# Passing the ends and beginnings of stages one block of 128 tokens at a time, merging by column blocks, and splitting weights in two steps

## The reference, cut to what matters

```python
for l in range(DEPTH):
    mod = silu(c) @ w_mod[l] + b_mod[l]                 # six rows of 1024: shift, scale, gate, twice
    h = rms_norm(x, g_mix_pre[l]) * (1 + sc_mix) + sh_mix
    y = hybrid_mixer(h, ...)                            # below
    x = x + gt_mix * rms_norm(y, g_mix_post[l])
    h = rms_norm(x, g_ffn_pre[l]) * (1 + sc_ffn) + sh_ffn
    y = swiglu(h, ...) if l % 2 == 0 else moe_swiglu(h, ...)   # dense; top 2 of 8 experts
    x = x + gt_ffn * rms_norm(y, g_ffn_post[l])

def hybrid_mixer(h, ...):
    proj = h @ w_in                 # 1024 x 5120: q, k, v of 8 stick-breaking heads, q, k, v of 8
                                    # MoBA heads, two gates of 1024 columns
    o_a = stick_breaking_attention(...) @ w_proj_sb
    o_b = moba_attention(...) @ w_proj_moba
    return (sigmoid(g_a) * o_a + sigmoid(g_b) * o_b) @ w_out
```

## Time and profile before

| | us |
|---|---|
| three runs: lowest, median, highest | 1754.01, 1759.09, 1759.86 |
| the profiled execution, its own time | 1758.54 |
| span in the profile | 1756.8 |
| mean granted share of TensorE's clock | 0.976 |

### The profile page before, as it was taken

The page is one execution under the profiler, slowest core; times in us unless marked ns, Lnnn a source line. Parts: engine busy times, 40 slices in busy tenths (PEclk is TensorE's granted clock), DMA queues, the critical chain, the costliest instruction groups (busy, mean ns, idle before and its releaser), DMA issues.

```text
span 1756.8 us, 23111 instructions
## 1 busy us (share of the span) xinstructions
PE 1667.5 (95%) x8014; PEld 1370.6 (78%) x8014; DVE 1386.9 (79%) x1260; ACT 1108.4 (63%) x965; POOL 62.9 (4%) x194
## 2 busy tenths in 40 slices
PE   6999879999979997799999999999999999999997
PEld 5977668878779776688788788788788788787885
DVE  7867867777685466588888888888888888888888
ACT  4656344334345564477777777777777777778775
POOL 0020010000000101400000000000000000000000
PEclk9999989999989999799999999999999999999998
DMA  9954647776556343189989899899899899899894
GB/s 385 394 203 180 247 165 284 273 266 254 215 210 256 134 149 139 51 309 372 350 342 371 309 358 376 316 365 374 317 373 371 297 373 368 321 375 358 325 370 165
DMA packets 72830, 512.05 MB, mean 291 GB/s; under 512 B 8963, under 2 KB 10188, under 8 KB 10828
## 3 DMA queue, kind: packets, MB, share of 16 engines
q1 hardware_dynamic: 72496, 511.26, 76.6%
q10 hardware_dynamic: 284, 0.13, 0.0%
HBM read 510.30 MB, written 1.06 MB: 291 GB/s over the span
## 4 chain that ended last, share of the span: by engine, by line
PE 85%; DVE 6%; ACT 4%; issue 3%; POOL 1%; DMA 1%; ACTq 0%; DVEq 0%; SPq 0%; POOLq 0%
PE ps L1231 26%; PE ps L1233 25%; PE ps L1232 25%; DVE wlo L291 3%; ACT whi L286 2%; PE ps L1564 2%; PE ps L1453 2%; DMA raw<-in_w_mod_units 1%; PE ps L1320 1%; DVE x L783 1%; ACT L286 1%; PE ps L1588 0%; DVE wide L1031 0%; PE ps L1340 0%; PE ps L1545 0%
## 5 line engine op out<-in xcount | busy, mean ns | idle before, releaser
L291 DVE TENSOR_TENSOR wlo<-raw,whi 128x2048 fp32r<-128x2048 f32 x436 | 993.7, 2290 | 231.2 <-ACT whi L286 229.1
L286 ACT ACTIVATE whi<-raw 128x2048 fp32r<-128x2048 f32 x436 | 833.7, 1916 | 294.0 <-PE ps L1233 293.4
L1231 PE MATMUL ps<-whi,hhi 128*128 128x512 f32 x1376 | 549.3, 399 | 15.3 <-DVE wlo L291 5.3
L1232 PE MATMUL ps<-whi,hlo 128*128 128x512 f32 x1376 | 539.8, 392 | 0.0
L1233 PE MATMUL ps<-wlo,hhi 128*128 128x512 f32 x1376 | 538.6, 391 | 0.0
L1231 PEld LDWEIGHTS ps<-whi,hhi 128*128 128x128 f32 x1376 | 260.5, 189 | 83.7 <-DVE wlo L291 14.2
L1233 PEld LDWEIGHTS ps<-wlo,hhi 128*128 128x128 f32 x1376 | 260.4, 189 | 55.9
L1232 PEld LDWEIGHTS ps<-whi,hlo 128*128 128x128 f32 x1376 | 260.7, 189 | 52.4 <-issue 1.0
L1231 PE MATMUL ps<-whi,ohi 128*128 128x512 f32 x624 | 250.5, 401 | 4.5 <-DVE gate L764 2.0
L1233 PE MATMUL ps<-wlo,ohi 128*128 128x512 f32 x624 | 244.5, 392 | 0.0
L1232 PE MATMUL ps<-whi,olo 128*128 128x512 f32 x624 | 243.8, 391 | 0.0
(11 more groups left out here) (214 smaller groups left out, 1062.4 us busy)
## 6 DMA issues: line engine op xcount, KB each, us to landing
raw<-in_w_moe SPq DMA_DIRECT2D x336, 1024.0 KB, 6.6
raw<-in_w_pre_moe SPq DMA_DIRECT2D x100, 1024.0 KB, 4.9
raw<-in_w_mod_units SPq DMA_DIRECT2D x48, 1024.0 KB, 5.4
x<-in_x SPq DMA_DIRECT2D x1, 1024.0 KB, 5.3
bias<-dist_scratch SPq DMA_DIRECT2D x1, 1024.0 KB, 7.9
out<-x SPq DMA_DIRECT2D x2, 512.0 KB, 2.7
condb<-in_c SPq DMA_DIRECT2D x1, 512.0 KB, 6.7
qk<-in_bucket_onehot ACTq DMA_DIRECT2D x1, 49.4 KB
```

The source lines that it names most:

```text
L286: nc.scalar.activation(whi[:, s % SPLIT, :], raw[:, slot(s), :], ACT.Copy).then_inc(hi_done, 1)
L291: nc.vector.tensor_tensor(wlo[:, s % SPLIT, :], raw[:, slot(s), :], whi[:, s % SPLIT, :].bitcast(F32), ALU.subtract).then_inc(lo_done, 1)
L1231: nc.tensor.matmul(out, a_hi, b_hi, start=first, stop=False, **kw)
L1232: nc.tensor.matmul(out, a_lo, b_hi, start=False, stop=False, **kw)
```

## The change

1. **Splits in two steps.** `split_hi` and `split_lo` do two instructions of 1024 columns instead of one of 2048. `hi_done` and `lo_done` count halves. PE's `use(s)` waits for the first half only, and a new `rest(s)` waits for the second in the middle of the unit's first pass (before the third of four k slices, or the second of two).
2. **Ends of stages by blocks of tokens.** Unit 24 is done for both blocks; then units 25, 26, 27 for block 0, and after that units 25, 26, 27 for block 1. The units of w_out are reordered (k half outside, column half inside). The last down products of the dense FFN are done likewise (`dense_end`), with three units' worth for block 0 and then for block 1; all three slots of whi and wlo are held until block 1 has used them.
3. **Beginnings of stages likewise.** `transposes(n, 0)`, then the first three units of the next stage for block 0, then `transposes(n, 1)`, then the same three units for block 1 (`phase_start`). For this mixer 1 takes its column blocks in the order 2, 6, 0, 1, 3, 4, 5, 7, 8, 9, in pairs of banks. Before the experts only the transposes are apart. ACT, DVE and POOL get one list each for a passage (`transition`), with split halves of the first units of the next stage placed between the pieces of work on each block.
4. **Merge by column blocks.** Units 20 and 21 are the two projections of column half 0, units 22 and 23 those of half 1. Half 0 is transposed after unit 22 and half 1 after unit 24. The four sigmoids are made one after each of the units 19 to 22. Attention steps stand nearer together (`STEP_AT`).
5. **Smaller.** Places of the mod loads in the ring; `gate_take` of the dense FFN at steps 1 and 2 instead of 1 and 3; squares are scaled by 1/32 in the instruction, so that POOL has one multiplication less; the residual add is one instruction of 1024 columns instead of two of 512.

```diff
     for s in range(FIRST, MOE0):
         order.append(("unit", s))
-        if (s < FFN0 and s in (8, 9, 10, 11, 12, 13, 15, 18, 21, 24, 25, 26)
-                or FFN0 <= s < FFN0 + 40 and (s - FFN0) % 2 == 0 or MIX1 < s <= MIX1 + 8):
+        f = s - FFN0
+        if (s in (8, 9, 10, 11, 12, 13, 15, 17, 18, 20, 21, 23)
+                or 0 < f < 38 and (f % 2 == 1 and f > 1 or f in (4, 6)) or MIX1 + 2 < s <= MIX1 + 10):
             order.append(("mod", next(mods)))
     assert next(mods, None) is None
     return order
...
+        def split_hi(act, s, r=0, halves=(0, 1)):
+            if 0 in halves:
+                act.wait_ge(raw_full[slot(s)], dma_value(s, r))
+                wait_at_least(act, unit_used, number(s, r) - SPLIT + 1)
+            for h in halves:
+                part = slice(h * D, (h + 1) * D)
+                nc.scalar.activation(whi[:, s % SPLIT, part], raw[:, slot(s), part], ACT.Copy).then_inc(hi_done, 1)
+
+        def split_lo(dve, s, r=0, halves=(0, 1)):
+            if 0 in halves:
+                wait_at_least(dve, unit_used, number(s, r) - SPLIT + 1)
+            for h in halves:
+                part = slice(h * D, (h + 1) * D)
+                dve.wait_ge(hi_done, number(s, r) * 2 + (h + 1))
+                nc.vector.tensor_tensor(wlo[:, s % SPLIT, part], raw[:, slot(s), part],
+                                        whi[:, s % SPLIT, part].bitcast(F32), ALU.subtract).then_inc(lo_done, 1)
 
...
+        HI = [0, 8, 12]
+        NEXT = [None, FFN0, MIX1, MOE0]
+        T_BANK = [None, (6, 4), (6, 4), (6, 0)]
+        Y_BANK = [(2, 4, 3, 5), (4, 5, 0, 1), (2, 4, 3, 5)]
+        ORDER = [list(range(BLK)), [2, 6, 0, 1, 3, 4, 5, 7, 8, 9]]
+        NEED = [[3, 4, 4, 4, 5, 5, 5, 5], [4, 4, 4, 4, 6, 6, 6, 6]]
+
+
+        STEP_AT = [16, 19, 22, 25, 28, 31, 33, 36, 38, 41]
+
...
+            def transition(q):
+
+                n = q + 1
+                square_y(q, 0)
+                square_y(q, 1)
+                split_hi(act, NEXT[n], halves=(0,))
+                square_x(n, 0)
+                split_hi(act, NEXT[n], halves=(1,))
+                split_hi(act, NEXT[n] + 1, halves=(0,))
+                if q != 1:
+                    square_y(q, 2)
+                hidden_a(n, 0)
+                if n < 3:
+                    hidden_hi(n, 0)
+                if q == 1:
+                    square_y(q, 2)
+                square_y(q, 3)
+                split_hi(act, NEXT[n] + 1, halves=(1,))
+                if n < 3:
+                    split_hi(act, NEXT[n] + 2)
+                square_x(n, 1)
+                hidden_a(n, 1)
+                if n < 3:
+                    hidden_hi(n, 1)
 
...
+            def transition(q):
+
+                n = q + 1
+                coefficients(n)
+                if q == 1:
+                    last_add(0)
+                    last_add(1)
+                gated_y(q, 0)
+                gated_y(q, 1)
+                residual(q, 0)
+                split_lo(dve, NEXT[n], halves=(0,))
+                normed(n, 0)
+                split_lo(dve, NEXT[n], halves=(1,))
+                hidden_b(n, 0)
+                if n < 3:
+                    hidden_lo(n, 0)
+                if q == 1:
+                    last_add(2)
+                    last_add(3)
+                split_lo(dve, NEXT[n] + 1, halves=(0,))
+                gated_y(q, 2)
+                gated_y(q, 3)
+                residual(q, 1)
+                split_lo(dve, NEXT[n] + 1, halves=(1,))
+                if n < 3:
+                    split_lo(dve, NEXT[n] + 2, halves=(0,))
+                normed(n, 1)
+                if n < 3:
+                    split_lo(dve, NEXT[n] + 2, halves=(1,))
+                hidden_b(n, 1)
+                if n < 3:
+                    hidden_lo(n, 1)
...
+                def merge_first(half):
+                    for c in range(C):
+                        dve.wait_ge(sig_done, 4 * l + 2 * half + 1)
+                        dve.wait_ge(unit_used, base + 21 + 2 * half)
+                        nc.vector.tensor_tensor(merged[:, c, half * NB:(half + 1) * NB], bank[4 * half + c][:],
+                                                gates[:, c, half * NB:(half + 1) * NB], ALU.mult).then_inc(mg_evac, 1)
+
+                def merge_second(half):
...
+                for u in range(MIX_UNITS - 2):
+                    if u == 25:
+                        merged_lo(1)
+                    if l and u or u >= FIRST - LEAD:
+                        stream_lo(dve, base + u + LEAD)
                     attention(2 * u)
                     attention(2 * u + 1)
...
+                    if u in (20, 22):
+                        merge_first((u - 20) // 2)
                     if u == 23:
+                        merged_lo(0)
+                    if u in (21, 23):
+                        merge_second((u - 21) // 2)
+                    if u == 22:
                         gate_diag(q)
...
-                    if t == 3 and j in (1, 3):
-                        gate_take(1, j // 2)
+                    if t == 3 and j in (1, 2):
+                        gate_take(1, j - 1)
...
+            def transition(q):
+                n = q + 1
                 for c in range(C):
+                    pool.wait_ge(ysq_done, 4 * q + 2 * c + 2)
+                    if c == 0 and q:
+                        pool.wait_ge(x_done, C * q)
+                    inv_rms(ry_done, ss[:, 2 * c:2 * c + 1], 4 + c, ss[:, 2 * c + 1:2 * c + 2])
+                    pool.wait_ge(sq_done, C * n + c)
+                    if c == 0:
+                        pool.wait_ge(xn_done, C * n)
+                    inv_rms(rstd_done, ss[:, 4 + c:5 + c], c)
+
...
             def use(s, r=0):
-                pe.wait_ge(lo_done, number(s, r) + 1)
+                pe.wait_ge(lo_done, number(s, r) * 2 + 1)
+
+            def rest(s, r=0):
+                pe.wait_ge(lo_done, number(s, r) * 2 + 2)
+
...
+            def rows_half(s, a_hi, a_lo, kcs, out, first, last, c):
+
+                w_hi, w_lo = unit(s, NB)
+                cs = slice(c * P, (c + 1) * P)
+                for k in range(4):
+                    if c == 0 and k == 2:
+                        rest(s)
+                    ins = three(out, a_hi[:, kcs + k, cs], a_lo[:, kcs + k, cs], w_hi[:, k, :], w_lo[:, k, :],
+                                first and k == 0, last and k == 3)
+                return ins
+
+            def phase_start(n, banks, added=0):
+
+                s0 = NEXT[n]
+                for c in range(C):
+                    for j in range(3):
+                        if c == 0:
+                            use(s0 + j)
+                            if j == 2:
+                                wait_at_least(pe, yadd_done, added)
+                        if j < 2:
+                            pe.wait_ge(hlo_done, HI[n] + 2 * c + j + 1)
+                        ins = rows_half(s0 + j, hhi, hlo, 4 * (j % 2), bank[banks[j] + c], j != 1, j == 1, c)
+                        if c:
+                            ins.then_inc(unit_used, 1)
+                    if c == 0:
+                        transposes(n, 1)
 
...
+                    if u in (22, 24):
+                        half = (u - 22) // 2
+                        for c in range(C):
+                            pe.wait_ge(mg_evac, 8 * l + 4 * half + 3 + c)
+                            if half:
+                                pe.wait_ge(mlo_done, 4 * l + c + 1)
                             for k in range(4):
                                 kk = 4 * half + k
-                                ins = nc.tensor.transpose(bank[[2, 3, 6, 4][i]][:, k * P:(k + 1) * P],
+                                ins = nc.tensor.transpose(bank[6 + c][:, k * P:(k + 1) * P],
                                                           merged[:, c, kk * P:(kk + 1) * P], ident[:])
                             ins.then_inc(mT_done, 1)
-                    if u == 25:
+                    if u == 24:
                         gate_rows(2 * l)
+                for c in range(C):
+                    for u in range(MIX_UNITS - 3, MIX_UNITS):
+                        s = base + u
+                        kh, half = divmod(u - 24, 2)
+                        if c == 0:
+                            use(s)
+                        if u == 25 and c == 0:
+                            pe.wait_ge(mg_evac, 8 * l + 6)
+                        if u == 26:
+                            pe.wait_ge(mlo_done, 4 * l + 3 + c)
+                        ins = rows_half(s, hhi, hlo, 4 * kh, bank[(4 if half else 2) + c], kh == 0, kh == 1, c)
+                        if c:
+                            ins.then_inc(unit_used, 1)
+                        elif u > 25:
+                            ins.then_inc(yh_done, 1)
...
+            def dense_end():
+
+                t = FBLK - 2
+                s0 = MIX1 - 4
+
+                def piece(s, c, part, b, half, first, last):
+                    w_hi, w_lo = unit(s, D)
```

(44 more changed lines are left out.)

554 lines of the change are left out of this document (260 added, 294 removed).

## The result

The changed kernel takes 1747.01 us (median of 6 runs, 1740.58 to 1751.61), the kernel before 1758.52 (median of 6). The ratio is 0.9938, interval 0.9914 to 0.9962: faster by 11.5 us, a third of the 34 that were forecast, and outside the range. The profiled execution of the changed kernel took 1751.61 us (span 1749.9), the slowest of its six and 4.6 above the median, so the traces show a gain of only 6.9 us, and more of the miss than the medians do.

What follows compares the result with a forecast made beforehand. The prediction took TensorE to bound the kernel (PE busy 1667.5 of 1756.8 us). Its terms summed to -34.1 us, taking 1758.54 to 1724.4 us; the range was 1710 to 1744.

Steps and rivals of the forecast that it cites:

- Moved loads: Mod loads and others issued by SP: same loads, slots freed no later, fewer mod loads before the first FFN units; 0 us.
- Dense FFN: Dense FFN: five block-boundary waits for adds go, -2.4 us; the second gate copy's wait and low clock go, -3.8 us.
- Splits: Experts: with halved splits, PE's waits for wlo all go; -7.0 us, bounds -7.7 and +15.
- Rival C: Every unit: the added mid-unit wait on PE costs 0.09 to 0.11 us, so slower, say 1768 us; chance 0.05.
- Start: Kernel's first unit: a half split starts 1.1 us sooner, part given back on VectorE; -0.6 us, bounds -1.1 and +0.5.
- Merge of layer 0: Merge in layer 0: PE's waits and low clock shrink from 6.7 us to 2.0 remaining; -4.7 us.
- End of mixer 0: Mixer 0's end to FFN start: block 0's chain covered, three waits and one low-clock spell remain; -4.8 us, bounds -8 and +2.
- rival B: Starts of two stages: broken streams stay at 1.2 GHz, each losing 3.4 us more; 1731.2 us, chance 0.12 within the forecast's.
- End of the FFN: FFN's end to mixer 1's start: 20.0 us lost before, 12.0 after; -8.0 us, bounds -11 and -1.
- Router: Mixer 1's end to router: logits start 12.7 us after y instead of 11.9; +0.8 us, bounds -2 and +3.
- D: Slots, attention or adds hold PE despite first halves and blocks; only merges and gate copy gain, 1746.4 us; chance 0.06.
- A: Stage ends and merges: waits only move, VectorE's small pieces and squeezed attention take the gain; 1741.3 us, chance 0.12.

## Why the prediction was wrong

**The step that failed** is the one of a sentence: "Moved loads. SP issues the same loads; each waits for a slot that is freed no later ...: 0." It counted what the loads cost SP and the ring, and left out what a load makes VectorE do, and where in VectorE's list. Each mod load is 2.3 us there, at a place that the ring sets. The ring line was in the diff, and the positions follow from it by one sum (6 + 6t + j). The ring alone puts 21 us on it, in both kernels; VectorE's order at the block boundaries alone gives back 15 of them, with the loads where they were. "Dense FFN", -2.4 - 3.8, was right but for this: -6.8 with the ring put back.

**Splits**, -7.0 forecast, -12.6 in the table from the first expert on. The stalls are gone as forecast, but a late unit costs more than its wait: of the 1.44 us that an expert became shorter, 1.04 are the two wlo stalls; in the excess of PE's start distances over 0.227 us, the rest is that fewer matmuls follow the first of a unit by 0.31 instead of 0.23 us. What stands behind the last expert gave 1.2 more. The reason was half right: earlier on VectorE, yes (by elimination); PE's start on a half, no, but for the first unit. Rival C is out.

**Start**, -0.6: VectorE's half split did come 1.1 us sooner (PE's wait 4.14 after 5.28), but what stands ahead of it came later by as much. By the same matmuls PE is 0.43 us ahead of the kernel before at 39 us and 0.65 behind at 60; in between a wait of 0.32 us for wlo (40.47) is new. Its cause was not tried; unit 16 of mixer 0 is reached between 132.2 and 133.7 us in these traces.

**Merge of layer 0**, -4.7 forecast, -1.2 measured. The merge itself is as forecast: PE waits 0.61 + 0.16 at 193.43 for merged_lo, the rest is gone, the low clock too. The term "squeezed attention" was priced at 1.3 and measured 2.2 at the scores, 1.7 for a spell of low clock (0.90 over 16.6 us) and 1.3 at unit 20. The first two go with the mods moved by one unit: the same oversight as in the FFN, and 3.1 us of the medians. With that the stretch gives -4.9. **Layer 1** has no mods there: -2.6 for -3.6, the difference again the 1.3 at unit 20: with the 0.8 for merged_lo 2.1 remain, where the prediction left 1.0.

**End of mixer 0**, -4.8 forecast, -2.9 measured. The three waits were overrated rather than not: 2.9, 2.2 and 2.3 us in place of 2.6, 3.4 and 2.6. But each of them had its own spell of low clock where one was counted (busy times by stretch, columns as in the earlier trace rows):

```profile
218.50:228.50 10.00, 7.30 (x28) 5.74 (x27) 8.54 (x12) 7.22 (x13) 3.21 (x5) 0.83 0.39 118
228.50:236.00 7.50, 5.48 (x23) 4.25 (x21) 3.51 (x2) 0.45 (x2) 2.14 (x5) 0.81 0.62 236
236.00:247.00 11.00, 8.87 (x32) 6.83 (x31) 5.66 (x9) 6.45 (x11) 0.00 (x0) 0.82 0.04 18
```

2 x (0.17 x 10 + 0.19 x 7.5 + 0.18 x 11) = 10.2 us at 1.2 GHz, 5.1 lost and not 1.7. That is rival B, in this stage alone. **End of the FFN**: -7.0 for -8.0, with one spell as counted (only 512 to 520 is low, 0.79).

**Router**, +0.8 forecast, +2.4 measured: normed beside GpSimd's zeroing was taken at the 2.38 us of the earlier trace rows (at this place it had been 2.73), and took 4.38, held behind six memsets and not two. Without them the stretch is 1.1 us shorter than before in the zeroing experiment, and within 0.1 of before in four of the five kernels that add the ring (1.2 shorter in the last).

Of the rivals none was it. D comes nearest in time (1746.4 for 1747.0), by luck: the halves and the first blocks do release PE as the change says. A (1741.3) named the pieces at the ends of stages, and these gave 9.9 of 12.8 us; it also named half of the merges' gain, and 3.8 of 8.3 us came, with a late olo at 143 us, at the end of unit 16. But 3.7 us of what is missing are the mod loads again; only the 1.3 at unit 20 of each layer may come from the nearer steps, which no run put back alone. The range (to 1744) had no room for the miss: the terms' own slow bounds add up to +19.5 us, which it didn't use, and the one term that was set to 0 looking only at SP was also the one without bounds.

## What to carry to other kernels

When a load moves in a ring, follow it to the engine that consumes it and write down what stands behind that work in the engine's list at the new place; a parity can be worth 20 us. Keep work that nobody waits for (here the mod products) behind the adds and the splits that PE waits for. When a copy and a subtraction pass a tile from one engine to another, halving both pays at the second engine even if the last consumer still waits for the whole.

## What was not expected of the hardware

Waits of the same length on PE are not always followed by low clock: of the five of 2.06 us in the changed kernel four were and one was not (1.00 at 411.5), of the five in the kernel with the early zeroing three were, and of the five of 2.77 us in the kernel with odd loads two were not. One spell costs 1.7 us, so a kernel with many waits near this length also scatters more: the six runs of the changed kernel span 11 us, the four with the ring put back 4.1 (the link between the two was only argued).

A tensor_scalar of VectorE beside GpSimd's memsets was not slowed in proportion: it was held, and ended 0.55 us after the memset that it had waited for. That was the last of four (2.38 us) at every place with four, and at the place with six the second in three kernels (2.73) and the last in three others (4.38), though it started 0.09 us behind the first in all of them. PE's first matmul after a wait that is already satisfied starts no later than any other: an expert of 42 units takes 124.4 us with one wait in each unit and with two.
